# Opening with the memory's weights split on ScalarE and VectorE, and the last projection with its eighth tile late

## The reference, cut to what matters

```python
def rms_norm(x, g):
    return x * lax.rsqrt(jnp.mean(x * x, axis=-1, keepdims=True) + EPS) * g

mem_n = rms_norm(mem, mem_norm)                  # 256 x 1024
for l in range(2):
    h = rms_norm(x, mix_norm[l])
    kv = mem_n @ w_mem_kv[l]                      # 1024 x 1024: keys 512, values 512
    mk, mv = kv[..., :512], kv[..., 512:]         # 4 heads of 128
    mixed, mq = attn_mixer(h, ...) if l == 0 else lru_mixer(h, ...)
    mo = softmax(mq @ mk^T / sqrt(128)) @ mv      # per head
    x = x + concat([mixed, mo]) @ w_out[l]
    x = x + relu(rms_norm(x, mlp_norm[l]) @ w_up[l]) ** 2 @ w_down[l]
...
merged = g_a * (y_a @ w_proj_a) + g_b * (y_b @ w_proj_b)
out = layernorm(ALPHA * x + merged @ w_out_2) * ln_g + ln_b
```

## Time and profile before

| | us |
|---|---|
| median of 3 runs | 3576.35 |
| lowest and highest | 3575.73 and 3578.29 |
| the profiled execution | 3579.53 |
| span of its instructions | 3577.7 |
| PE busy | 3496.0 (98%) |
| DVE busy | 1788.3 (50%) |
| ACT busy | 971.5 (27%) |
| POOL busy | 1057.3 (30%) |

### The profile page before, as it was taken

The page is one execution under the profiler, slowest core; times in us unless marked ns, Lnnn a source line. Parts: engine busy times, 40 slices in busy tenths (PEclk is TensorE's granted clock), DMA queues, the critical chain, the costliest instruction groups (busy, mean ns, idle before and its releaser), DMA issues.

```text
span 3577.7 us, 44443 instructions
## 1 busy us (share of the span) xinstructions
PE 3496.0 (98%) x16486; PEld 2885.4 (81%) x16486; DVE 1788.3 (50%) x1937; ACT 971.5 (27%) x1582; POOL 1057.3 (30%) x588
## 2 busy tenths in 40 slices
PE   7999999999999999999999999999999999999999
PEld 6878888888888887767888888888788888878877
DVE  6446661633433356885264333435746456454454
ACT  3347760201010114764130101012333233202011
POOL 0120033333333330014233333333344344323350
PEclk9999999999999999999999999999999999999999
DMA  4110012111111112111211111111211111111241
GB/s 178 45 40 12 23 39 82 65 47 47 47 49 51 47 47 103 44 47 48 71 65 47 53 47 47 47 48 52 91 65 41 59 59 42 62 44 62 96 133 68
DMA packets 58519, 211.03 MB, mean 59 GB/s; under 512 B 6672, under 2 KB 11280, under 8 KB 56752
## 3 DMA queue, kind: packets, MB, share of 16 engines
q1 hardware_dynamic: 47504, 159.67, 13.4%
q10 hardware_dynamic: 10912, 50.01, 3.7%
HBM read 186.32 MB, written 22.02 MB: 58 GB/s over the span
## 4 chain that ended last, share of the span: by engine, by line
PE 88%; DVE 8%; issue 2%; ACT 2%; DMA 0%; DVEq 0%; ACTq 0%; POOL 0%; SPq 0%; POOLq 0%
PE G L570 70%; PE G L1137 2%; PE G L770 2%; PE AUX L832 2%; PE AUX L1016 2%; PE AUX L822 1%; PE G L659 1%; PE AUX L812 1%; PE AUX L699 1%; PE G L619 1%; PE G L622 1%; DVE xc L2150 1%; PE AUX L1098 1%; DVE ig L2175 1%; PE AUX L683 0%
## 5 line engine op out<-in xcount | busy, mean ns | idle before, releaser
L570 PE MATMUL G<-Hhi,whi 128*128 128x512 f32 x2576 | 1033.5, 401 | 10.7 <-issue 3.4
L570 PE MATMUL G<-Hhi,wlo 128*128 128x512 f32 x2576 | 1006.7, 391 | 0.0
L570 PE MATMUL G<-Hlo,whi 128*128 128x512 f32 x2576 | 1006.5, 391 | 0.0
L457 POOL CAST whi<-wraw 128x1024 fp32r<-128x1024 f32 (+1 forms) x255 | 273.1, 1071 | 2252.1 <-PE G L570 1081.4
L459 POOL TENSOR_TENSOR wlo<-wraw,whi 128x1024 fp32r<-128x1024 f32 (+1 forms) x255 | 626.9, 2459 | 20.4
L570 PEld LDWEIGHTS G<-Hhi,whi 128*128 128x128 f32 x2576 | 486.0, 189 | 119.1 <-issue 11.1
L570 PEld LDWEIGHTS G<-Hlo,whi 128*128 128x128 f32 x2576 | 486.0, 189 | 103.4 <-issue 6.0
L570 PEld LDWEIGHTS G<-Hhi,wlo 128*128 128x128 f32 x2576 | 485.6, 188 | 102.5
L570 PE MATMUL G<-Ulo,whi 128*128 128x512 f32 x1024 | 398.4, 389 | 0.0
L570 PE MATMUL G<-Uhi,wlo 128*128 128x512 f32 x1024 | 398.4, 389 | 0.0
L570 PE MATMUL G<-Uhi,whi 128*128 128x512 f32 x1024 | 398.4, 389 | 0.0
(11 more groups left out here) (354 smaller groups left out, 4709.9 us busy)
## 6 DMA issues: line engine op xcount, KB each, us to landing
wraw<-wjobs SPq DMA_DIRECT2D x292, 512.0 KB, 3.3
scratch<-X ACTq DMA_DIRECT2D x2, 4096.0 KB, 14.4
gate_tiles<-gate_st ACTq DMA_DIRECT2D x16, 512.0 KB, 4.5
T<-gate_tiles ACTq DMA_DIRECT2D x16, 512.0 KB, 3.4
X<-xT ACTq DMA_DIRECT2D x1, 4096.0 KB, 16.3
X<-xT ACTq DMA_DIRECT2D x4, 1024.0 KB, 4.9
X<-scratch ACTq DMA_DIRECT2D x4, 1024.0 KB, 4.8
X<-scratch SPq DMA_DIRECT2D x4, 1024.0 KB, 11.0
```

What stands on the lines that cost most here:

```text
L457: pool.tensor_copy(whi[:, par, 0:kt], wraw[:, par, 0:kt]).then_inc(w_hi, 1)
L570: mm = pe.matmul(G[:, par if psum is None else psum, cols], w[:, par, k, :], x[:, k, cols], start=(i == 0 and j == 0), stop=(i == kt - 1 a ...
```

## The change

**Opening.** The first 16 weight tiles are loaded into four buffers of their own (`mw_raw`), ACT casts each (`mw_hi`, three slots and a fourth for tile 2), DVE subtracts (`mw_lo`), and PE multiplies in three terms like everywhere else. The memory is split without its norm, times `mem_norm` only (`mem_hi`, `mem_lo`). Its root and reciprocal come while PE works and are applied when the products are read from PSUM: on the keys by DVE, on the values by ACT. A value job now covers two feature tiles of 512 output columns. `x` is likewise split without its norm. Its sums are made in the middle of the first query job (`sums_of_tokens`, at part 12 of 16), per token as a column (`rtok`, applied in the scores' scale and on `vals`) and as a row (`rstd_0`, applied on `sin` and `cos`). `X` is loaded in two halves by SyncE between the weights. The angles, the reciprocal of `rstd_0` and most of `decay_factors` move into DVE's stream of `mem_attention(0)`, one piece in each step from the third on. Pool's stream in the opening is empty but for the splits of the query jobs.

**Last projection.** Products 0 and 1 first run over seven tiles each and then over the eighth of each. Pool's second half of the weight splits waits for `both_lo` to be complete (`s_lo` at 24). `X2` comes in eight transfers of 512 KB, and the last two weight loads stand behind them. The last block's final operation and its output transfer are cut in two.

```diff
@@ sync
+            load_memory(0)
+            sp.dma_start(mraw[:], memT).then_inc(mem_in, 16)
+            load_memory(1)
+            sp.wait_ge(mem_in, 16)
+            load_memory(2)
+            load_memory(3)
+            load_x(0)
+            for n in range(4, MEM_JOBS):
+                load_memory(n)            # waits for mw_split n - 3
+                if n == 6:
+                    load_x(1)
...
             sp.wait_ge(job_done, START["out"])
-            for c in range(4):
-                cols = slice(c * 2 * P, (c + 1) * 2 * P)
-                sp.dma_start(X2[:, :, cols], scratch[0][:, :, cols]).then_inc(x2_back[c], 16)
+            for half in range(2):
+                for c in range(4):
+                    rows, cols = slice(4 * half, 4 * half + 4), slice(c * 2 * P, (c + 1) * 2 * P)
+                    sp.dma_start(X2[:, rows, cols], scratch[0][:, rows, cols]).then_inc((x_back if half else x2_back)[c], 16)
+            for n in range(N_JOBS - 2, N_JOBS):
+                load(n)
@@ gpsimd
+                if half:
+                    pool.wait_ge(job_done, START["out"])
+                    pool.wait_ge(s_lo, 3 * KT)
@@ tensor
+            def keys(l, m):
+                n = START[f"mem{l}k"] + m
+                if l:
+                    pe.wait_ge(evac["dve"], 2 + m + 1)
+                pe.wait_ge(mw_split, n + 1)
+                for k in range(KT):
+                    if n == 0:
+                        pe.wait_ge(norm_s["lo"], tiles_before("nmem") + k + 1)
+                    for j, (w, x) in enumerate(((mw_hi, mem_hi), (mw_hi, mem_lo), (mw_lo, mem_hi))):
+                        mm = pe.matmul(key_bank(m), w[mw_slot(n)][:, k, :], x[:, k, :], start=(k == 0 and j == 0),
+                                       stop=(k == KT - 1 and j == 2))
+                mm.then_inc(job_done, 1)
...
+                for u in range(2):
+                    product(u, 0, KT - 1)
+                for u in range(2):
+                    product(u, KT - 1, KT)
@@ scalar, start()
+                for k in range(1, 6):
+                    cast(5 + k)
+                    high(k)
+                act.wait_ge(norm_s["var"], 1)
+                values_out(0)
...
+                act.wait_ge(norm_s["ssq"], 2)
+                act.activation(rtok[:, 0, :], AUX[:, 1, 0:NBLK], ACT.Sqrt, bias=eps_col, scale=1.0 / D).then_inc(norm_s["r"], 1)
+                act.wait_ge(norm_s["lo"], tiles_before("nmix0") + KT)
+                chain.link(act.activation(rstd_0[:], AUX[:, 2:4, :].rearrange("p a n -> p (a n)"), ACT.Sqrt, bias=eps_col,
+                                          scale=1.0 / D))
                 act.wait_ge(l_dec, 1)
                 act.activation(decay_c[:, 16:32], decay_c[:, 0:16], ACT.Exp, scale=-1.0).then_inc(l_de, 1)
+                act.wait_ge(evac["act"], 2 + 8)
+                act.wait_ge(evac["dve"], 2 + 8)
                 act.dma_start(kv_tiles[0], ...)
                 act.dma_start(kv_tiles[1], ...)
+                act.dma_start(mixed[:, 2, :].bitcast(I32), pos).then_inc(mem_in, 16)
@@ vector, mem_attention
+                    if l == 0 and 2 <= v < 22:
+                        angle_step(v - 2)
+                    elif l == 0 and 22 <= v < 26:
+                        part = slice((v - 22) * MEM, (v - 21) * MEM)
+                        dve.wait_ge(act_chain, 1)
+                        chain.link(dve.reciprocal(rstd_0[:, part], rstd_0[:, part]))
+                    elif l == 0 and v == 26:
+                        decay_end()
@@ vector, window
+                for t in (sin, cos):
+                    chain.link(dve.tensor_tensor(t[:], t[:], rstd_0[:], ALU.mult))
```

More of the change, by code:

```diff
@@ new lines, in values @@
+            def values(l):
+                if l:
+                    pe.wait_ge(evac["dve"], 2 + 4 + 2)
+                for u in range(4):
+                    n = START[f"mem{l}v"] + u
+                    pe.wait_ge(mw_split, n + 1)
+                    for k in (2 * u, 2 * u + 1):
+                        for t in range(2):
+                            tokens = slice(t * P, (t + 1) * P)
+                            for j, (x, w) in enumerate(((mem_hi, mw_hi), (mem_lo, mw_hi), (mem_hi, mw_lo))):
+                                rows = w[mw_slot(n)][:].rearrange("p a n -> p (a n)")[:, k % 2 * 512:(k % 2 + 1) * 512]
+                                mm = pe.matmul(G[:, l, t * 512:(t + 1) * 512], x[:, k, tokens], rows,
+                                               start=(k == 0 and j == 0), stop=(k == KT - 1 and j == 2))
+                    mm.then_inc(job_done, 1)
@@ L1122, in project_tokens, with product @@
             def project_tokens():
-                def product(u):
+                def product(u, first=0, last=KT):
                     half, t = u // NBLK, u % NBLK
-                    if half == 0 and t < 2:
+                    if first == 0 and half == 0 and t < 2:
                         pe.wait_ge(evac["dve"], 2 + BASE["out"]["dve"] - 1 + t)
@@ L1129, in product @@
                         pe.wait_ge(o_ev, u - 1)
-                    for k in range(KT):
+                    for k in range(first, last):
                         if u == 0:
@@ L1144, in turn_residual @@
                         pe.wait_ge(o_rc, 1)
[L1145 to L1146 removed]
+                    if t % 2 == 0:
+                        pe.wait_ge(*((x_back[t // 2], 48) if half else (x2_back[t // 2], 16)))
                     if u >= 4:
@@ new lines, in start @@
+                cast(0)
+                act.wait_ge(mem_in, 16)
+                for k in range(KT):
+                    act.activation(mem_hi[:, k, :], mraw[:, k, :], ACT.Copy, scale=vcol("mem_norm", k)).then_inc(norm_s["hi"], 1)
+                cast(1)
+                cast(2)
+                for k in range(4):
+                    square("nmem", k, mraw, MEM)
+                cast(3)
+                for k in range(4, KT):
+                    square("nmem", k, mraw, MEM)
+                cast(4)
@@ new lines, in start @@
+                high(0)
+                cast(5)
+                act.wait_ge(norm_s["ssq"], 1)
+                act.activation(rstd_m[:], AUX[:, 0, 0:MEM + 2], ACT.Sqrt, bias=eps_col, scale=1.0 / D).then_inc(norm_s["r"], 1)
+                for k in range(1, 6):
[3 more added lines that the diff above has]
+                values_out(0)
+                for k in range(6, KT):
+                    cast(5 + k)
+                    high(k)
@@ new lines, in start @@
+                for k in range(3):
+                    cast(13 + k)
+                    square("nmix0", k, X, S)
+                for k in range(3, KT):
+                    square("nmix0", k, X, S)
+                values_out(1)
+                act.wait_ge(norm_s["ssq"], 2)
[3 more added lines that the diff above has]
+                                          scale=1.0 / D))
@@ L2542 @@
     a = {k: np.asarray(v) for k, v in inputs.items()}
-    jobs = weight_jobs(a["w_mem_kv"][0]) + weight_jobs(a["w_mem_kv"][1])
+    jobs = []
+    for w in a["w_mem_kv"]:
+        jobs += weight_jobs(w[:, :512]) + list(w[:, 512:].reshape(4, 2, P, 512).transpose(0, 2, 1, 3).reshape(4, P, KT * P))
     for l in range(2):
```

428 lines of the change are left out of this document (239 added, 189 removed).

## The result

The changed kernel takes 3544.56 us (median of 4 runs, 3539.65 to 3545.73), the kernel before 3577.32 (4 runs, 3575.73 to 3582.52): a ratio of 0.9903, 95% interval 0.9886 to 0.992. The gain is 32.8 us by the medians and 34.2 by the two profiled executions (spans 3577.7 and 3543.5). The forecast was 3546.7: 2.1 us too long by the time, and 3.1 us too small by the gain (29.7), as it started from the 3576.35 us of three earlier runs.

What follows compares the result with a forecast made beforehand. The prediction took PE, busy 98% of the span, as the bound. Opening -26.6, attention +4.5 and last projection -7.6 sum to -29.7 us, taking 3576.35 to 3546.7 us, range 3538 to 3563.

Steps and rivals of the forecast that it cites:

- Opening: Kernel start up to `turn(0)`: it comes at 78.5 instead of 105.1 us, a gain of 26.6 us.
- The step from the earlier trace to 0.12 us for 256 columns: Opening's key products: a 256-column fp32r matmul costs 0.12 us, taken from 384 columns at 0.18 and 512 at 0.229.
- PE and DVE arrive together: Opening, at 66.4 us: DVE's last square and PE's 12 parts of `mq0` end together; cheapening either gains little.
- The walk: Opening: queues followed operation by operation, 60.2 us without waits, plus 2 for arrivals and held slots, 2 per Pool split.
- The new wait in front of the evacuation: Opening: ACT's four DMA issues delay the evacuation of `mq0` from 72 to 75, a new wait of 3 us.
- Attention: Memory attention: DVE's added steps cost 4.5 us, between 1.8 without Pool and 6.3 with three splits; bounds 1.5 and 7.5.
- `window()`: Two multiplications, 2.4 us, ahead of the first key rotation cost nothing, hidden by a 3.67 us wait for its transfer.
- Last projection: Last projection: product 2 starts at 3479.7 instead of 3487.25, a gain of 7.6 us; bounds 5.5 and 8.2.
- The step that names the eighth tile as the cause: Last projection: the first product pauses for `both_lo`'s eighth tile, ready at 3475.99; changed, 3472; `X2` is next in line.
- (A): Rival, opening: PE stays at 1.2 GHz throughout, `turn(0)` at 99.4, kernel 3567.5 us; chance 0.08.
- (B): Rival, opening: 256-column fp32r products cost the float32 price, 0.446 us; `turn(0)` at 140.5, kernel 3608 us; chance 0.04.
- (C): Rival, memory attention: DVE paces it, 36.3 us of added work lands on the path, kernel 3578.5 us; chance 0.03.

Runs made afterwards that it cites:

- experiment 1: Changed kernel with its last projection as before (product order, no hold on Pool, X2 in four parts behind the weights); median 3553.32 us.
- experiment 3: Changed kernel with Pool's second split of a query weight waiting until the tokens' squares are summed; median 3543.51 us.
- experiment 4: Changed kernel with the product of the memory's low part in the value jobs left out or issued twice; medians 3540.61 and 3551.22 us.
- x2_old: Changed kernel with only X2's transfer back at its old place and size; median 3558.14 us.
- experiment 2: Changed kernel with ACT's four DMA issues ahead of its wait for the token sums instead of behind the roots; median 3543.0 us.
- experiment 9: Changed kernel with two of the four rstd_0 reciprocals in the opening, two in steps 25 and 26, decay's end in step 27; median 3540.31 us.
- experiment 5: Changed kernel with only X2's transfer back at its old place and size, four parts behind the last weight loads; median 3558.14 us.
- experiment 6: Changed kernel with X2 still early in eight parts, but first two products whole and in order and Pool not held; median 3552.43 us.
- experiment 10: The kernel before, unchanged, profiled a second time; span 3575.2 us against 3577.7.
- experiment 7: Changed kernel with only Pool's hold removed; median 3544.95 us.
- pe_light: Changed kernel with the product of the memory's low part left out of the value jobs; median 3540.61 us.
- combined: Changed kernel with the edits of experiment 2, experiment 3 and experiment 9, and token sums behind 9 parts of mq0 instead of 12; median 3538.24 us.
- issue_early: Changed kernel with ACT's four DMA issues ahead of its wait for the token sums; median 3543.0 us.
- pool_late: Changed kernel with Pool's second split of a query weight behind the sums of the tokens' squares; median 3543.51 us.
- pe_heavy: Changed kernel with the product of the memory's low part issued twice in the value jobs; median 3551.22 us.

## Why the prediction came out as it did

**The direction, the two places and their sizes were right**, and experiment 1 shows that they are separate. The forecast gain fell 3.1 us short by the medians, and the terms say where.

**Opening: 26.6 forecast, 26.2 measured** (27.5 against the second profile of before). The step from the earlier trace rows to 0.12 us for 256 columns was exact. The end of the products (58 forecast, 58.4 measured), the last square summed (66.4; 66.82) and "PE and DVE arrive together" (experiments 3 and 4) held too. Several steps inside it were off and cancelled.

- The first subtraction was to come at 7.4 and came at 8.97, as the tables landed at 7.8, not at 6.23 as in the earlier trace rows. Why is not shown: SyncE's loads of memory and weights now run beside them, but other loads did before, too. The walk had 2 us for late transfers and held slots, and this start took most of them.
- The sums of the tokens were put at 2.8 us. They took 3.8 at full clock (`x2_old`: 66.39 to 70.17) and 4.6 in the changed kernel's profile.
- The new wait in front of the evacuation was forecast at 3 us, from 72 to 75. At full clock its part by the issues is 1.5 (experiment 2). The sum laid the four issues, 2.7 us, behind the table load and the small exponential. In the trace they run beside them: the table load takes 72.76 to 74.04, and the first issue starts at 72.84.
- In the profile of the changed kernel `mq0`'s last matmul ended at about 75.05 (74.65 + 0.40) and only 0.8 us of wait were left, as the sums and the parts behind them ran partly at a clock of 0.50. The 1.1 us that I had added for slow clock belonged there, not at the start.
- From the evacuation to `turn(0)` it took 3.1 us, not 2.4.

One reading of the kernel before was too simple. Its chain from 20 to 85 is not the products throughout: up to 31.16 it is mostly DVE's sums for the norm of `x`, and from 43.77 to 48.05 it is a weight load (the kernel before, start, length, what):

```profile
23.30 1.23 DVE acc L1774
...
43.77 4.28 DMA wraw<-wjobs
```

The sum does not suffer, as it took only the time of `turn(0)` from that trace.

**Attention: +4.5 forecast, +2.4 measured.** The term is two things that I had not kept apart. From first to last result the 32 steps became 4.0 us longer (79.99 to 83.98). Of that 2.9 lie in the steps with the reciprocals and the decay, as forecast, and experiment 9 takes back 2.6 of them. About 1.1 lie at the short steps 8 and 16, each time with an angle step behind Pool's subtraction. That these steps are the cause is argued from the timeline alone, no run tested it. Against it, the way from `turn(0)` to the first result became 1.5 us shorter (4.56 to 3.01), since the clock there was 0.58 before and is 1.00 now. That was missing from the sum. Where the 4.0 come from was partly misjudged as well: I had 1.8 without Pool and the rest from Pool. In fact only two angle steps met Pool, 2.10 us instead of 1.22 each, 1.8 us of DVE's time in all, and the lead of 3 us that I had subtracted in steps 22 to 26 was smaller: those five steps became 4.9 us longer (5.4 forecast without a lead), and 2.0 us came back in the step behind them, 1.29 us instead of 3.29.

**`window()`: 0 forecast.** The two multiplications took 1.22 us each and DVE still waited 1.15 us for the transfer that the earlier trace rows show at 3.67. The cover held.

**Last projection: 7.6 forecast, 7.5 measured**, 8.7 against the second profile of before. The step that names the eighth tile as the cause, with `X2` "the next in line", was right for that one profile only. Experiments 5, 6 and 10 show two bounds of nearly the same size, one behind the other. The forecast came out because the change removes both, and in part by luck: the prediction checked `X2` against the first profile alone. Had the change kept `X2`'s place and held Pool, the same argument would still have promised a gain, and the kernel would have been 13.6 us slower than the changed one (experiment 5). That Pool's hold would also shift SyncE's loads stood nowhere in my text. And DVE's two operations do not need the hold: once the order gives 9.6 us of cover, 3.3 and 3.1 us beside Pool fit (experiment 7).

**The last block in halves: 0 forecast, 0.4 at most measured** (0.43 against the first profile, 0.15 against the second, for all that lies behind product 2).

**The middle, -2.6 us, was not forecast**, and most of it is no part of the change: the second profile of before has a middle 4.8 us shorter than the first (3272.5 against 3277.2), and the changed kernel's lies between (3274.7). This is also the answer to the 3.1 us that the total was off by: beside the two seen in the attention's term, it is of the size by which one kernel differs from itself (spans of 3577.7 and 3575.2).

**The rivals.** (A), a slow clock through the opening, did not come: the products from 15.1 on went at 0.12 us. The Trainium skill (TensorE: Matmul & The Clock Gate, section HAM oscillation) tells of a kernel that waits several us for its data between short bursts of matmuls and falls back to the half clock at every wait. This opening is no such case: from 10.74 to 66.76 PE had no idle time, so the trace cannot speak for or against the rule. Nearest to it is `pe_light`, with waits of 2.29 us at 50.9 and 1.94 us at 63.5, and a clock of 0.50 to 0.60 from 66 to 73. (B), a float32 price for 256 columns, and (C), an attention paced by DVE throughout, did not come either; (C) is true of the five steps with the reciprocals and the decay, of 32.

## What to carry to other kernels

When a stall is removed, ask of each transfer and each queue behind it when it would have been ready without the stall, and do it on more than one profile: here the eighth tile and `X2` were late by nearly the same amount, and whether `X2` showed at all differed between two executions of one kernel. A hold on one engine is also a hold on every load that waits for its buffers; follow it into the DMA queue. Where two engines arrive together, making one of them cheaper gains next to nothing: 3.3 us less on DVE started the next step 0.55 us earlier, 7.3 us less on PE 1.5 us earlier. What `combined` gained in the opening came with PE having parts to do while ACT makes the roots, and with the issues moved to where ACT is idle.

## What the runs showed of the hardware

- In the changed kernel the first 20 matmuls of 256 columns went at 0.213 us from start to start (0.35 the first) and the following ones at 0.12. That is half of the 0.43 us that a 512-column matmul took at a granted clock of 0.50 in the kernel before (six between 89.94 and 92.08), so PE was at the low level, 1.2 GHz, though the stretch from 11 to 15 us has a granted clock of 1.00 in the profile. So the granted clock of the profile does not show PE's first slow stretch here.
- PE's clock dropped in nearly continuous work in the changed kernel, behind 16 records of single columns (L698), with 0.10 us of idle time ahead of them. The stretches, columns as above:

```profile
69.00:70.00 1.00, 1.00 (x3) 0.44 (x2) 0.00 (x0) 0.00 (x0) 0.00 (x0) 0.84 0.00 0
70.00:71.00 1.00, 1.00 (x3) 0.33 (x1) 0.00 (x0) 0.00 (x0) 0.00 (x0) 0.50 0.00 0
```

  It is no accident of this execution. In twelve profiles with these sums, PE waited for DVE's last sum in eight, for 0.07 to 1.94 us, and in seven of them the clock fell to 0.50 behind the sums (`issue_early`, with 0.10 us, is the exception). In the four in which the sums followed the matmuls at once (`pool_late`, `x2_old`, `pe_heavy`, `combined`) it stayed at 1.00 through sums and parts. Whether the short wait decides it is not shown.
- An addition or subtraction with two inputs on 1024 columns took 1.23 us alone and 3.1 to 3.4 beside Pool's subtraction. The Trainium skill (SBUF — State Buffer, section SBUF: two separate sides) states an exclusive lock between the two engines for such operations: the one that starts second waits until the first is done. The trace agrees. Here the price is 2.1 us of waiting, close to the 2.4 us of Pool's own operation; twice in the attention DVE paid only 0.9 us, and Pool's operation took 3.3 us instead of 2.4.
